# A two-layer transformer kernel on one core: the router laid into the last dense block, and ends reordered

## The reference

```python
# layer 1, mixture of experts: 32 experts in 4 groups, two experts for a token
xf = _rmsnorm(h, norm_g)
p_group = softmax(xf @ w_group + b_group); g_sel = argmax(p_group)
e_logits = (xf @ w_expert + b_expert)[own group]; top_p, top_i = top_k(softmax(e_logits), 2)
h = h + sum over the two experts: gate * (silu(x @ w_gate[e]) * (x @ w_up[e])) @ w_down[e]
# layer 2
z = rmsnorm(x, g_in) @ w_in           # q, k, v, gates of three branches
kv = rmsnorm(mem, g_mem) @ w_mem_kv   # its second half is the block "xv2"
u = gates[0] * (ya @ w_up_moba) + gates[1] * (yb @ w_up_dsa) + gates[2] * (yc @ w_up_cross)
out = rmsnorm(x + u @ w_out, g_final)
```

## Time and profile before

| what | us |
|---|---|
| median of 3 runs | 1044.28 (1042.95 to 1044.6) |
| profiled execution, its own time | 1044.35 |
| span of the profile | 1042.6 |
| PE busy | 864.6 (83%) |
| DVE busy | 458.3 (44%) |
| ACT busy | 327.3 (31%) |
| moved by DMA | 292.13 MB, mean 280 GB/s |

### The profile page before, as it was taken

The page is one execution under the profiler, slowest core; times in us unless marked ns, Lnnn a source line. Parts: engine busy times, 40 slices in busy tenths (PEclk is TensorE's granted clock), DMA queues, the critical chain, the costliest instruction groups (busy, mean ns, idle before and its releaser), DMA issues.

```text
span 1042.6 us, 13537 instructions
## 1 busy us (share of the span) xinstructions
PE 864.6 (83%) x5461; PEld 598.3 (57%) x5461; DVE 458.3 (44%) x850; ACT 327.3 (31%) x526; POOL 23.6 (2%) x34
## 2 busy tenths in 40 slices
PE   8999999999986575666566665747999999999996
PEld 7877888898732131212113131311787899999985
DVE  5668766674602020201102021000776788565683
ACT  4655654764110010000000000001434645545332
POOL 1030010100000000000000000000000000000000
PEclk9999999999998787988879788788999999999999
DMA  9552455585999999999999999999355344344340
GB/s 303 186 169 82 162 205 206 182 336 189 363 405 421 422 421 421 421 419 422 422 422 422 421 420 421 421 421 399 122 189 174 123 161 162 125 159 147 138 162 40
DMA packets 73982, 292.13 MB, mean 280 GB/s; under 512 B 6498, under 2 KB 6980, under 8 KB 50884
## 3 DMA queue, kind: packets, MB, share of 16 engines
q1 hardware_dynamic: 71860, 289.54, 72.0%
q10 hardware_dynamic: 2064, 1.79, 0.5%
HBM read 290.25 MB, written 1.05 MB: 279 GB/s over the span
## 4 chain that ended last, share of the span: by engine, by line
issue 30%; PE 30%; DMA 25%; SPq 8%; DVE 4%; ACT 2%; ACTq 0%; POOL 0%; DVEq 0%; POOLq 0%
DMA ring<-in_w_e_down 12%; DMA ring<-in_w_e_gate 8%; SPq L614 6%; PE bank L2657 5%; DMA ring<-in_w_e_up 5%; PE bank L2264 5%; PE bank L2266 5%; PE bank L2265 5%; PE bank L2676 3%; SPq L629 2%; DVE ring_rounded L1349 2%; PE bank L2632 1%; PE bank L2201 1%; ACT ring_rounded L846 1%; PE bank L2704 1%
## 5 line engine op out<-in xcount | busy, mean ns | idle before, releaser
L1349 DVE TENSOR_TENSOR ring_rounded<-ring,ring_rounded 128x2048 fp32r<-128x2048 f32 x80 | 183.3, 2291 | 130.4 <-ACT ring_rounded L846 130.1
L846 ACT ACTIVATE ring_rounded<-ring 128x2048 fp32r<-128x2048 f32 x80 | 153.2, 1915 | 192.0 <-PE bank L2266 190.9
L2657 PE MATMUL bank<-ring,main 128*32 128x512 f32 x768 | 113.4, 744 | 72.0 <-DMA ring<-in_w_e_up 52.8
L2265 PE MATMUL bank<-ring_rounded 128*128 128x256 f32 (+1 forms) x512 | 161.8, 316 | 0.0
L2266 PE MATMUL bank<-ring_rounded 128*128 128x512 f32 x352 | 137.4, 390 | 0.0
L2657 PEld LDWEIGHTS bank<-ring,main 128*32 128x32 f32 x768 | 28.8, 132 | 147.2 <-issue 89.3
L2264 PE MATMUL bank<-uT_rounded,ring_rounded 128*128 128x256 f32 x352 | 101.7, 289 | 0.4 <-issue 0.4
L2265 PEld LDWEIGHTS bank<-ring_rounded 128*128 128x128 f32 x512 | 97.5, 190 | 6.0
L2266 PE MATMUL bank<-uT_rounded,ring_rounded 128*128 128x256 f32 x352 | 99.5, 283 | 0.0
L2676 PE MATMUL bank<-ring,main 128*32 128x512 f32 x384 | 65.6, 843 | 40.9 <-DMA ring<-in_w_e_down 40.1
L1874 DVE TENSOR_TENSOR h<-bank,h 128x512 f32<-128x512 f32 x32 | 22.0, 691 | 174.2 <-PE bank L2704 174.2
(11 more groups left out here) (296 smaller groups left out, 1259.2 us busy)
## 6 DMA issues: line engine op xcount, KB each, us to landing
ring<-in_w_in SPq DMA_DIRECT2D x46, 1024.0 KB, 5.0
ring<-in_w_e_gate SPq DMA_DIRECT2D x46, 1024.0 KB, 25.7
ring<-in_w_e_up SPq DMA_DIRECT2D x46, 1024.0 KB, 26.3
ring<-in_w_e_down SPq DMA_DIRECT2D x40, 1024.0 KB, 25.8
main<-in_w_e_up SPq DMA_DIRECT2D x12, 1024.0 KB, 25.5
main<-in_w_e_gate SPq DMA_DIRECT2D x12, 1024.0 KB, 25.4
main<-in_w_e_down SPq DMA_DIRECT2D x12, 1024.0 KB, 25.7
ring<-in_w_ckv SPq DMA_DIRECT2D x8, 1024.0 KB, 5.1
```

Source lines behind the costliest of these rows:

```text
L846: a.activation(rounded(hi_half(h)), raw_half(name, h), ACT.Copy).then_inc(hi_made, 1)
L1349: v.tensor_tensor(rounded(raw), raw, as_f32(hi_half(h)), ALU.subtract).then_inc(split_made, 1)
L2265: mm(dst, left[0], right[1], start=False, stop=False, skip_group_check=True)
L2657: last = mm(bank[2 + part][on, :], xg3[:, h * (KC // 2) + k, on], weight_unit(unit_buffer(p, u), e, KC)[:, k, :], start=h + k == 0, stop=h ...
```

## The change

Six places are edited.

1. **Router.** PE no longer runs transposes, logits and then xv2. It starts xv2's first quarter right behind co1 and lays the logits of one chunk behind each step; h2T2 and h2T3 are transposed ahead of the second quarter and their chunks' logits laid behind its second and third step. The rank products stand ahead of the last quarter, not of the second half. On DVE the second half's split and the second norm_tokens come ahead of the logits, and the copies of h2T2 and h2T3 go to ACT. On SP the expert piece that waits for the logits is issued behind the first quarter's pair. One staged MiB is loaded by one transfer and not by two.
2. **Last expert unit.** Its second row chunk is loaded in two column halves (12 transfers, not 8), PE waits for each, and 13 products of constants (keep_busy) stand between the first chunk and the second.
3. **Start of layer two.** DVE makes the low parts of h3T0 and h3T1 between the two halves of the adds, and h3T2 and h3T3 are transposed inside block iq.
4. **Block mv.** Its second half is split behind the last two index scores, on ACT and DVE.
5. **Blocks up2 and out0.** The first half of out0 gets a place of its own (raw in mem2T, high part in main), is loaded ahead of up2 and split ahead of up2. The second half of up2 is split by DVE in the middle of the adds of branch 1.
6. **End.** Squares, gains and root work by column half and token tile; the gain is multiplied in before the root is there; the last tile's scaling and its store are shared by DVE with SP and by ACT.

On PE at the router, where co1 ends, the order before is the following.

The diff, cut to its core:

```diff
         def raw_half(name, h):
+            if (name, h) == ("out0", 0):
+                return mem2T
             at = (2 * DENSE_BLOCKS.index(name) + h) % RAW_HALVES * HALF
             return ring[:, at:at + HALF]
 
-        def hi_half(h):
+        def hi_half(name, h):
+            if (name, h) == ("out0", 0):
+                return main[:, 6400:8448]
             return ring[:, 2 * SLOT + h * HALF:2 * SLOT + (h + 1) * HALF]
 
+        def split_place(name, h):
+
+            if (name, h) == ("out0", 0):
+                return 2 * DENSE_BLOCKS.index("up2") + 1
+            return 2 * DENSE_BLOCKS.index(name) + h + (2 if name == "up2" else 1)
...
                     if last and u == UNITS - 1:
-                        for k in range(2):
+                        for n, (k, at) in enumerate(((0, slice(0, D)), (1, slice(0, 512)), (1, slice(512, D)))):
                             for i, e in enumerate(experts):
-                                sp.dma_start(weight_unit(unit_buffer(p, u), i, chunks)[:, k:k + 1, :],
-                                             w_of[e, :, 2 + k:3 + k, :]).then_inc(last_landed[k], 16)
+                                sp.dma_start(weight_unit(unit_buffer(p, u), i, chunks)[:, k:k + 1, at],
+                                             w_of[e, :, 2 + k:3 + k, at]).then_inc(last_landed[n], 16)
...
-            wait_filled(sp, "logits")
-            load_unit(2, (GROUP - 1,), up_w_of, 0, at=GROUP - 1)
...
+                    if half + q == 0:
+                        wait_filled(sp, "logits")
+                        load_unit(2, (GROUP - 1,), up_w_of, 0, at=GROUP - 1)
...
-                load_dense(name)
+                if name == "up2":
+                    load_dense("out0", [0])
+                load_dense(name, [1] if name == "out0" else range(2))
...
             square_rows("h2", h, normed, "co")
             split_hi("xv2", [1])
+            for c2 in (2, 3):
+                copy(f"h2T{c2}", uT_chunks(c2))
             act.wait_ge(router_args, 1)
...
                 if name == "il1_2":
-                    split_hi("mv")
+                    split_hi("mv", [0])
                 relu_bank(name)
+            split_hi("mv", [1])
             split_hi("mg", [0])
...
             split_hi("up1", [1])
+            split_hi("out0", [0])
             split_hi("up2")
-            split_hi("out0", [0])
...
-            square_rows("final", h, normed, "out")
+            for n in range(2 * TT):
+                j, t = n // TT, n % TT
+                wait_drained(act, f"out{j}_{t}")
+                a.activation(lo_b[:, n * 512:(n + 1) * 512], h[:, t, j * 512:(j + 1) * 512], ACT.Square,
+                             accum_out=final_sq[:, 2 * t + j:2 * t + j + 1]).then_inc(final_squared, 1)
+            act.wait_ge(rstd_ready, len(NORMS) + 1)
+            act.wait_ge(final_gained, 4)
+            at = NORM_AT["final"][1] + 1
+            a.activation(normed[:, 1, 0:512], normed[:, 1, 0:512], ACT.Copy, scale=rstd[:, at:at + 1])\
+                .then_inc(last_half_ready, 1)
+            act.wait_ge(last_half_ready, 1)
+            act.dma_start(token_major(out[0])[:, 1, 0:512], normed[:, 1, 0:512]).then_inc(out_stored, 16)
...
             in_order(dve, row_squared, ROW_NORMS, "h2")
             mean("h2", D)
-            for c2 in (2, 3):
-                copy(f"h2T{c2}", uT_chunks(c2))
             wait_rstd(dve, "h2")
             _, row0, _ = NORM_AT["h2"]
...
             norm_tokens(0)
+            split_lo("xv2", [1])
+            norm_tokens(1)
...
-            split_lo("xv2", [1])
...
-            norm_tokens(1)
...
+
+            def first_of_second_layer():
+                split_lo("iq", [0])
+                norm_T("h3", lo_a, uT_flat, "g_in_2", (0, 1))
+
             for p in range(2):
                 gathered_high(moe, last_quad + p)
                 dve_quad(moe, last_quad + p, None if p else QUADS - 1,
-                         (lambda: split_lo("iq", [0])) if p else None)
+                         first_of_second_layer if p else None)
             mark(after_experts, 1)
             dve.wait_ge(moe.added, last_quad * 4 + 12)
-
-
-            norm_T("h3", lo_a, uT_flat, "g_in_2", (0, 1))
             split_lo("iq", [1])
             norm_T("h3", lo_a, uT_flat, "g_in_2", (2, 3))
...
             for name in RELUS[2:]:
                 if name == "il1_2":
-                    split_lo("mv")
+                    split_lo("mv", [0])
                 score_bank(name)
+            split_lo("mv", [1])
             rope_tensor("mk", mk_tok)
...
+            split_lo("out0", [0])
             split_lo("up2", [0])
...
             for c in range(4):
+                if c == 2:
+                    split_lo("up2", [1])
                 link(add_branch(1, c))
-            split_lo("up2", [1])
-            split_lo("out0", [0])
...
-            add_to_h("out", 0.5, ("out1", None))
-            in_order(dve, row_squared, ROW_NORMS, "final")
...
+            split_lo("out1")
...
+            def add_out(j, t):
+                done(f"out{j}_{t}", v.scalar_tensor_tensor(hs, wait_filled(dve, f"out{j}_{t}")[:, :], 0.5, hs,
+                                                           ALU.mult, ALU.add))
+
+            def gain_out(j, t):
+                wait_drained(dve, f"out{j}_{t}")
+                v.scalar_tensor_tensor(normed[:, t, at], h[:, t, at], float(D) ** 0.5, wide_gain[:, at],
+                                       ALU.mult, ALU.mult).then_inc(final_gained, 1)
+
+            def sum_out(t):
+                dve.wait_ge(final_squared, 3 + t)
+                v.tensor_scalar(mean_sq[:, lo + t:lo + t + 1], final_sq[:, 2 * t:2 * t + 1],
+                                final_sq[:, 2 * t + 1:2 * t + 2], D * EPS, ALU.add, ALU.add).then_inc(means_ready, 1)
+
+            def scale_out(t):
+                x = normed[:, t, 512 * t:D]
+                v.tensor_scalar(x, x, rstd[:, lo + t:lo + t + 1], None, ALU.mult).then_inc(out_ready, 1)
+
+            for t in range(TT):
+                add_out(0, t)
-            _, lo, _ = NORM_AT["final"]
-            for t in range(TT):
-                v.scalar_tensor_tensor(normed[:, t, :], h[:, t, :], rstd[:, lo + t:lo + t + 1],
-                                       wide_gain[:, :], ALU.mult, ALU.mult).then_inc(out_ready, 1)
+            for t in range(TT):
+                gain_out(0, t)
+            add_out(1, 0)
+            gain_out(1, 0)
+            sum_out(0)
+            add_out(1, 1)
+            gain_out(1, 1)
+            scale_out(0)
+            sum_out(1)
+            scale_out(1)
...
+            def moving_by_quarters(name, x, before_quarter, behind_step):
...
+            def logits_of(k):
                 for t in range(TT):
+                    last = mm(b[:, t * w:(t + 1) * w], uT[:, k, t * P:(t + 1) * P], w_router[:, k, :],
+                              start=t + k == 0, stop=k == KC - 1, skip_group_check=True)
+                return last
+
+            def router_before(h, q):
+                if (h, q) == (0, 1):
+                    both_drained("co1_0", "co1_1")
+                    turn(["h2T2", "h2T3"], h_tok, 2)
+                elif (h, q) == (1, 1):
                     pe.wait_ge(router_step, 1)
...
-            moving_by_quarters("xv2", parts(mem2T, mem2_lo), rank_tokens)
-
+            def logits_behind(h, q, step):
+                if (h, q) == (0, 0):
+                    if step == 0:
+                        pe.wait_ge(router_scaled, 1)
+                        both_drained("h2T0", "h2T1")
+                        wait_free("logits")
+                    logits_of(step)
+                elif (h, q) == (0, 1) and step in (1, 2):
+                    wait_drained(pe, f"h2T{step + 1}")
+                    logits_of(2 * step + 2)
+                    last = logits_of(2 * step + 3)
+                    if step == 2:
+                        full("logits", last)
+
+            moving_by_quarters("xv2", parts(mem2T, mem2_lo), router_before, logits_behind)
...
-                        if final and h and half == 0:
-                            pe.wait_ge(last_landed[k], 16 * GROUP)
+                        if final and h and (half, k) == (0, 1):
+                            keep_busy(bank[0], 13)
+                        if final and h and (k == 1 or half == 0):
+                            pe.wait_ge(last_landed[k + k * half], 16 * GROUP)
...
-            for half in range(2):
-                pe.wait_ge(moe.added, of_quad(last_pair, 1, 4, 6 + 2 * half))
-                turn([f"h3T{2 * half}", f"h3T{2 * half + 1}"], h_tok, 2 * half)
-
-            moving("iq", stream, lambda h: both_drained(f"h3T{2 * h}", f"h3T{2 * h + 1}"))
+            pe.wait_ge(moe.added, of_quad(last_pair, 1, 4, 6))
+            turn(["h3T0", "h3T1"], h_tok)
+
+            def turn_second_half(h, t):
+                if (h, t) == (0, 1):
+                    pe.wait_ge(moe.added, of_quad(last_pair, 1, 4, 8))
```

(3 more changed lines are left out.)

120 lines of the change are left out of this document (67 added, 53 removed).

## The result

| | median | runs |
|---|---|---|
| before | 1043.83 us | 1042.95 to 1044.6, 4 runs |
| changed | 1032.57 us | 1031.56 to 1035.26, 4 runs |
| ratio | 0.9896 | 95% interval 0.9876 to 0.9917 |

Measured against the base of 1044.35 us from which the forecast was taken, the forecast is a ratio of 0.9914 and its range 0.9891 to 0.9953; the measured ratio lies inside that. The profiled execution took 1032.58 us (span 1030.6), against 1044.35 (1042.6): 11.8 us less, where 9.0 were forecast.

What follows compares the result with a forecast made beforehand. It took the loop as bound by its weight transfers and the second layer by PE. From 1044.35 us, 2.2 + 1.9 − 0.15 + 0.8 + 2.3 + 1.9 = 8.95 gave 1035.4 us, range 1033.0 to 1039.4.

Steps and rivals of the forecast that it cites:

- the router's term: Router and start of the loop: the transfer-bound loop gains 2.2 us, bounds 0 and 2.6.
- gather: At the router: the first gather starts at 274.0 and not at 276.58, 2.5 us earlier.
- last unit: Last expert unit: the scatter starts 1.9 us earlier (0.9 to 2.7).
- start of layer two: From the scatter's start through iq: a loss of 0.15 us (−1.9 to +0.8).
- mv: Block mv, second layer: PE's 1.6 us wait for ACT's relu shrinks, gain 0.8 us (0 to 1.6).
- up2, out0: Blocks up2 and out0: two of three PE waits go, 1.0 us is left, gain 2.3 us (1.0 to 2.9).
- end: Behind the last product: less DVE work behind the last root, gain 1.9 us (1.0 to 2.5).
- the ranks' wait: At the router: PE's wait for router_step ahead of the rank products is about nothing (269.9 against 270.3).
- (a): Before iq: the clock falls in PE's new 2.5 us wait, price 1.7 us, 1037.1 us; chance 0.15.
- (b): Loop starts no earlier: low rate belongs to the pieces, or router's chain is late; 2.2 lost, 1037.6 us; chance 0.14.
- (c): DVE is the bound at the end: the gains 2.3 and 1.9 shrink by half, 1037.5 us; chance 0.14.
- (d): Slower: the loop's transfer queue runs dry in each of eight quads, 1051 us at 2 us a quad; chance 0.04.

Runs made afterwards that it cites:

- first pair held back: The changed kernel, but the first pair of pieces waits again behind the logits and the piece for uT: 1035.22 us, ratio 0.9920.
- the one with the delay: The kernel before with 14 products of constants between the logits and the first quarter of xv2: 1045.79 us, ratio 1.0025.
- before again: The kernel before, unchanged, in one more profiled execution: 1041.57 us.
- 8 and 14 constants: The changed kernel with 8 products of constants in the last expert unit, not 13, and 14 more before iq: 1032.26 us, ratio 0.9901.

## Why the prediction was wrong, and where it was right

**The step that failed** is the size of the router's term, in the last paragraph on the router: "Bounds: 0 (the low rate is of the pieces themselves) and 2.6. I take 2.2". Counted from the transposes, u4 came 5.2 us earlier in the profiled pair (460.0 to 454.8), twice the upper bound; of the three parts measured alone it is also the one whose interval (2.3 to 4.9) lies above its forecast. Two things were wrong in it.
First, the bound took the gather as the measure of the stream. The text had the first pair going out at 261.9 in place of 267.26 and the queue losing 4.6 us, and then capped the gain at what PE gains. The queue is fed by the first pair too, and that alone is worth 1.4 us in rate, and 2.3 to 2.5 at u4, with the gather unmoved (first pair held back). Against an execution of before whose clock held, the whole step gives 2.4 us in rate (390 to 410) and 2.7 in u4, so most of the step is the first pair.
Second, the 1.7 us of slow clock were taken as a trait of the kernel. They are in three of the seven profiles that have before's order at the router (the one with the delay among them). Where they are, they reach the stream: 1.5 us of rate between before and before again. The profiled pair had the fall, so the forecast was right to count it there; the next execution need not have it. The remaining 1.3 us of the 5.2 is not in the rate of those 50 us; it lies in the rest of the stream and in the landing of the last units. What sets it stays open.

**By terms**, profiled pair: 

| term | forecast | measured | |
|---|---|---|---|
| gather | 2.5 | 2.7 | of it 1.6 clock, 1.2 order |
| router, start of loop (u4) | 2.2 | 5.2 | 2.7 against before, again |
| last unit | 1.9 | 0.6 | before's 13.7 hold 1.7 of slow clock |
| start of layer two | −0.15 | +0.2 | 1.1 less to iq, 0.9 back in it |
| mv | 0.8 | 0.7 | 1.6 to 0.8 of wait |
| up2, out0 | 2.3 | 2.4 | waits left 0.6 and 0.2 |
| end | 1.9 | 2.1 | 2.48 to 0.49 behind the root |

The terms below the gather's row, and the 0.7 by which the changed kernel's transposes in co1 came earlier, make the 12.0 us of the spans; the own times differ by 0.2 less. Against before, again (1041.57), the changed execution is 9.0 faster, and the sum was 8.95; that is partly luck, since the last unit was 1.3 short, the other steps together 1.1 better, the transposes stood 0.5 earlier, and what an execution takes beyond its span was 0.3 longer.

The miss itself is small beside these: 0.4 us below the range, while the base of 1044.35 stands 0.5 above the median of 1043.83. And the range's lower edge was set narrower than its own terms allow: their upper bounds, 2.6 + 2.7 + 0.8 + 1.6 + 2.9 + 2.5, sum to 13.1 us, which is 1031.3.

**What was right.** No fall at the router in any of the seven executions with the new order, where three of seven with the old one have it; the ranks' wait is at most 0.1 (DVE's mark at 268.94, PE there at 269.14); iq 6.8 behind the scatter (7 forecast); waits before out0 0.8 in all (about 1 forecast); half a microsecond behind the root. The rate from 258 to 290 us was forecast near 390 and is 407, which is the failed step seen elsewhere.
**The last unit** was mis-sized: the 13 constants were laid against a first chunk that starts 5.1 us behind u4 (718.59 and 713.48). In the changed kernel u4's products ran longer at half clock and it starts 6.3 behind; the constants outlasted the last landing by 0.8 us, and the first half's products stood behind them. The rest of the term was a reading of one profile: 1.7 of its 1.9 us are the slow clock behind the wait, which two of seven executions with the old unit do not have.
**Rivals.** (a), the clock in the wait before iq, did not come in the changed kernel's two profiles, but did in three of the four other executions with that wait and no constants in it, at 1.5 us (price on record 1.7). It is a live cost of this version. Its premise, that waits of 3.2 us let the clock fall, holds in five executions and fails in two. (b) is refuted by the rate, (c) by the waits, (d) by 420 GB/s in the loop as before.

A candidate for a better version is the one with 8 and 14 constants: it has the lowest median, 1032.26 against 1033.12 on the same chip, but the intervals don't part them.

## What to carry to other kernels

Where a stream bounds what follows, the gain of an edit ahead of it is counted in the issues of its transfers, each by how much earlier it goes out and whether the queue was dry, not by the engine that issues the last of them. A short fall of the clock in one profile is a draw, not a trait: look at a second execution before a term is built on it, and keep its cost in the range with both signs. The forecast leaned on such a fall twice, at the router and in the last unit, and both were missing in some executions of the same code. Filler work in a wait is sized by the latest end that the work ahead can have, or it outlasts the wait.

## What the runs showed of the hardware

The same code on the same data ran at 1.00 or 0.50 behind the narrow logits, and the unlike executions differ by 2.3 to 2.8 us in all. In the last unit the clock fell behind a wait of 3.2 us in five executions and held in two (16 records in 3.0 to 3.6 us against 1.92). The Trainium skill ("TensorE: Matmul & The Clock Gate", Part 1) says that the number of slow products at a kernel's start varies from run to run. The profiles here agree: near the start, between 12 and 16 us, the clock was at half in three executions and not in the others, and at 262 us the same holds of the kernel before (9 products against 16 in the same 3.42 us).

Products of constants are no protection by themselves: 14 of them right behind the logits ran into the slow clock (28 records in 5.00 us, against 3.29 at full clock). In the last unit 13 ran at full clock, but there it also held once without any.

The share of the DMA engines shows a queue that is empty, and hides one that is only short of work. In 3 us around the late pair it was 0.67 for 175 GB/s, and 0.17 for 29 GB/s in 2 us of the kernel with the delay; but over longer stretches 0.98 and 1.01 stood for 359 and 407 GB/s, and 0.99 for 398. There the rate, not the share, told how much transfer time was unused.
